# Seven block products in place of eight in four gate-and-up column groups of two feed-forward stages

## What is computed

```python
def swiglu(h, w_in, w_out):
    g, u = split_cols(h @ w_in, (D_FF, D_FF))
    return (jax.nn.silu(g) * u) @ w_out

for layer in range(DEPTH):                     # DEPTH = 2
    g = ln_gains[layer]
    x = x + 0.5 * swiglu(rms_norm(x, g[0]), ffn1_w_in[layer], ffn1_w_out[layer])
```

## Time and profile before

| | before |
|---|---|
| median of three runs | 1864.86 us (1864.74 to 1865.78) |
| the profiled execution: time, span | 1865.1 us, 1862.7 us |
| busy: PE, PE weight loads | 1857.9 us (100%), 1623.7 us (87%) |
| busy: VectorE, ScalarE, POOL | 1310.3 us (70%), 1119.3 us (60%), 369.0 us (20%) |
| TensorE's granted clock | full in all 40 slices |
| first feed-forward stage of the change | its down product begins at 883 us, its groups some 110 us earlier |

### The profile page before, as it was taken

One profiled execution on the slowest core, in us unless ns is written; L12 is line 12 of the kernel. 1 busy time (PEld: TensorE's weight loads), 2 busy tenths in 40 slices (PEclk: granted clock), 3 DMA queues, 4 the chain that ended last, 5 costly groups with the idle time before them and its releaser, 6 DMA issues.

```text
span 1862.7 us, 25413 instructions
## 1 busy us (share of the span) xinstructions
PE 1857.9 (100%) x9293; PEld 1623.7 (87%) x9293; DVE 1310.3 (70%) x1949; ACT 1119.3 (60%) x1678; POOL 369.0 (20%) x606
## 2 busy tenths in 40 slices
PE   9999999999999999999999999999999999999999
PEld 8888988888889888888888889888888888899888
DVE  6776776667777776666577886776666578977664
ACT  6776655557766655555468785654555467765553
POOL 2101233111001431122103001531122111102320
PEclk9999999999999999999999999999999999999999
DMA  9767789878578997798765567997798788758984
GB/s 316 236 186 229 222 258 299 260 233 253 166 221 242 292 287 232 219 272 255 238 180 191 174 191 204 281 274 237 225 255 252 227 265 242 216 157 232 255 258 138
DMA packets 289803, 436.43 MB, mean 234 GB/s; under 512 B 25548, under 2 KB 170416, under 8 KB 289424
## 3 DMA queue, kind: packets, MB, share of 16 engines
q1 hardware_dynamic: 260384, 352.41, 61.9%
q0 software_dynamic: 28832, 82.07, 16.3%
q10 hardware_dynamic: 464, 0.34, 0.1%
HBM read 396.43 MB, written 38.29 MB: 233 GB/s over the span
## 4 chain that ended last, share of the span: by engine, by line
PE 99%; DMA 0%; DVE 0%; SPq 0%; ACT 0%; issue 0%; ACTq 0%
PE M L1081 31%; PE M L1083 31%; PE M L1082 31%; PE AUX L1124 1%; PE AUX L1138 0%; PE AUX L1252 0%; DMA RAW<-in_w_in 0%; PE AUX L1244 0%; PE AUX L1242 0%; PE AUX L1279 0%; PE AUX L1167 0%; PE AUX L1295 0%; PE AUX L1323 0%; PE AUX L1296 0%; PE AUX L1297 0%; PE AUX L1324 0%
## 5 line engine op out<-in xcount | busy, mean ns | idle before, releaser
L1647 DVE TENSOR_TENSOR WL<-RAW,WH 128x1024 fp32r<-128x1024 f32 (+1 forms) x669 | 810.8, 1217 | 383.5 <-ACT WH L1358 380.9
L1358 ACT ACTIVATE WH<-RAW 128x1024 fp32r<-128x1024 f32 (+1 forms) x670 | 705.0, 1055 | 518.8 <-PE M L1083 469.7
L1081 PE MATMUL M<-WH,Bh 128*128 128x512 f32 (+1 forms) x1820 | 691.3, 380 | 0.6 <-ACT TMP L1401 0.3
L1082 PE MATMUL M<-WL,Bh 128*128 128x512 f32 (+1 forms) x1820 | 683.1, 375 | 0.0
L1083 PE MATMUL M<-WH,Bl 128*128 128x512 f32 (+1 forms) x1820 | 683.1, 375 | 0.0
L1081 PEld LDWEIGHTS M<-WH,Bh 128*128 128x128 f32 x1820 | 344.2, 189 | 50.6 <-issue 4.2
L1083 PEld LDWEIGHTS M<-WH,Bl 128*128 128x128 f32 x1820 | 344.2, 189 | 47.1
L1082 PEld LDWEIGHTS M<-WL,Bh 128*128 128x128 f32 x1820 | 344.4, 189 | 44.7
L1396 ACT ACTIVATE AS<-M,KEEP 128x256 f32<-128x256 f32 x132 | 55.3, 470 | 80.3 <-PE M L1083 78.7
L1081 PE MATMUL M<-WH,MTh 128*128 128x512 f32 x128 | 51.0, 398 | 0.0
L1082 PE MATMUL M<-WL,MTh 128*128 128x512 f32 x128 | 48.5, 379 | 0.0
(11 more groups left out here) (534 smaller groups left out, 2886.9 us busy)
## 6 DMA issues: line engine op xcount, KB each, us to landing
RAW<-in_ffn_w_in SPq DMA_DIRECT2D x352, 256.0 KB, 4.2
RAW<-in_w_in SPq DMA_DIRECT2D x103, 512.0 KB, 4.8
RAW<-in_w_gate_up SPq DMA_DIRECT2D x176, 256.0 KB, 4.4
RAW<-in_ffn_w_out SPq DMA_DIRECT2D x88, 512.0 KB, 4.6
RAW<-in_w_down SPq DMA_DIRECT2D x44, 512.0 KB, 4.9
RAW<-in_x_w_kv SPq DMA_DIRECT2D x32, 512.0 KB, 4.6
RAW<-in_even_w_in SPq DMA_DIRECT2D x24, 512.0 KB, 4.5
RAW<-in_odd_w_in SPq DMA_DIRECT2D x24, 512.0 KB, 5.4
```

Of the source, the lines that this page charges most:

```text
L1081: e.matmul(out, s.hi, wh, start=s.at0, stop=False)
L1082: e.matmul(out, s.hi, wl, start=False, stop=False)
L1358: e.activation(hi, raw, ACT.Copy).then_inc(k.w_hi, 1)
L1647: e.tensor_tensor(lo, raw, hi.bitcast(F32), ALU.subtract).then_inc(k.w_lo, 1)
```

## The change

In both stages, groups 6 and 9 of the eleven are computed with seven block products in place of eight. The tokens times features (2 x 2 blocks of 128 tokens by 512 features) and the weights (2 x 2 blocks of 512 features by 256 columns, gate or up) are combined by sums in float32; each product is 128 tokens by 512 features by 256 columns. With all its parts:

- **Weight plan.** `add_mixed` lays group 5's four plain units ("o") and group 6's seven product units ("p") in turn, by `TURNS`; the same for groups 8 and 9. A product unit is four feature blocks by 256 columns and has no load of its own (`None`). TensorE makes 12 matmuls of 256 columns with it (`sp`, `sp2`), into banks of `AUX`.
- **Weight blocks.** SP loads the four blocks of the group into `TMP` (rows 0 to 7), 256 KB a transfer, two transfers after each of the four units that stand before the first product. The first of them waits for the last token sum (first pass) or for the subtraction of the last product unit of the pass before (second pass).
- **Weight sums.** POOL makes T1 to T4 (`tsum`), 1024 elements a partition each, into `KX` and over blocks no longer needed. T1 waits for all eight transfers, T2 for T1 and the subtraction of the first product unit, T4 for T2 and that of the fourth.
- **Token sums.** Once a stage VectorE adds high and low parts back together (2048 elements), POOL makes four sums of 512, ScalarE and VectorE their parts, in rows of `GA` and a new tile `SUM`.
- **Product sums.** `sv0` (ScalarE copy), `sv1` (three on VectorE), `sv2` (one) add up the products; silu and gating of the group then read these instead of `M`.
- **Conversions.** The seven product units are converted from blocks and sums, by the same two operations as before: eleven units in two groups where there were eight.
- The results of groups 8 and 9 are turned into `GA` only after the last product has been used, since the token sums lie there.

```diff
+    def add_mixed(name, w):
+        v = w.rearrange("(k p) (two f) -> p k two f", p=P, two=2)
+        for c in ORDER:
+            if not isinstance(c, tuple):
+                add(name, w, [gu[c]], pairs=True)
+                continue
+            plain, own = c
...
+            for x in TURNS:
+                if x[0] == "o":
+                    q = int(x[1])
+                    units.append((2, 512, v[:, 2 * q:2 * q + 2, :, 256 * plain:256 * plain + 256]))
+                else:
+                    seven["at"].append(len(units))
+                    units.append((4, 256, None))
...
+ORDER = (0, 1, 2, 3, 4, (5, 6), 7, (8, 9), 10)
+TURNS = "p0 o0 p1 p2 o1 p3 p4 o2 p5 o3 p6".split()
+BLOCKS = "B11 B21 B22 T1 T3 T2 T4".split()
...
+        for j, (at, kind) in enumerate(((-7.5, "T1"), (-7.0, "T3"), (-3.0, "T2"), (3.5, "T4"))):
+            s = self.add("tsum", start + at)
...
+        elif s.kind in ("sp", "sp2"):
...
+            for kk in range(4):
+                wh, wl = (woven(x[:, h, 256 * kk:256 * kk + 256]) for x in (p.WH, p.WL))
+                e.matmul(out, xh[kk], wh, start=kk == 0, stop=False)
+                e.matmul(out, xh[kk], wl, start=False, stop=False)
+                i = e.matmul(out, xl[kk], wh, start=False, stop=kk == 3)
+            i.then_inc(k.w_used, 1)
...
+                if j < 3:
+                    e.wait_ge(k.d_sr, 128 * (n + 1))
+                else:
+                    e.wait_ge(k.t_made, 4 * n + j - 2)
+                e.wait_ge(k.w_used, s.u - NHL + 1)
+                e.activation(in_four(p.WH[:, h, 0:s.size]), block(p, BLOCKS[j]), ACT.Copy).then_inc(k.w_hi, 1)
...
+            e.tensor_tensor(pair(p.TMP[8]), pair(p.AUX[x1.bank][:, :]), twice(p.JK[:, 0:256]), ALU.add).then_inc(k.aux_out[x1.bank], 1)
...
+            e.tensor_tensor(pair(p.VT), pair(p.AUX[x3.bank][:, :]), twice(p.TMP[8][:, 256:512]), ALU.add).then_inc(k.part_sum, 1)
...
+            e.tensor_tensor(p.FLAT[:, 512:768], p.AUX[x3.bank][:, 0:256], p.VT[:, 256:512], ALU.add).then_inc(k.aux_out[x3.bank], 1)
+        elif s.kind == "sv2":
...
+        elif s.kind == "tsum":
+            at = p.sevens[s.i]["at"]
+            x, y = {"T1": ("B12", "B11"), "T3": ("B22", "B12"), "T2": ("B22", "T1"), "T4": ("B21", "T2")}[s.what]
+            if s.what == "T1":
+                e.wait_ge(k.d_sr, 128 * (s.i + 1))
+            elif s.what == "T2":
+                e.wait_ge(k.t_made, 4 * s.i + 1)
+                e.wait_ge(k.w_lo, at[0] + 1)
+            elif s.what == "T4":
+                e.wait_ge(k.t_made, 4 * s.i + 3)
+                e.wait_ge(k.w_lo, at[3] + 1)
+            e.tensor_tensor(block(p, s.what), block(p, x), block(p, y), ALU.subtract).then_inc(k.t_made, 1)
...
         weights(i)
+        if i in p.blocks_at:
+            n, q = p.blocks_at[i]
+            x = p.sevens[n]
+            if q == 0 and n % 2 == 0:
+                e.wait_ge(k.s_lo, 4 * (n // 2) + 4)
+            elif q == 0:
+                e.wait_ge(k.w_lo, p.sevens[n - 1]["at"][6] + 1)
+            for j in range(2):
+                e.dma_start(p.ROWS[:, 2 * q + j, :].rearrange("p (two f) -> p two f", two=2), x["src"][q][:, j]).then_inc(k.d_sr, 16)
```

More of the change, by code:

```diff
@@ L531, in residual, with token_sums, seven_products, ffn @@
             x.after = self.n_unit
-    def ffn(self, gate, down, lab_in, lab_mid, scale, gain, lab_next, A, HB, final=False, gated=False, early=None):
+    def token_sums(self, lab, A, extra):
+        n = self.n_seven // 2
+        s = self.add("sums", self.now + 0.6)
+        s.i, s.done = n, self.n_unit
+        s.makers = []
+        for kt in range(KD):
+            if self.made[lab, kt] not in s.makers:
+                s.makers.append(self.made[lab, kt])
+        s.hi, s.lo = ([x[:, 16 + 2 * i:18 + 2 * i, :].rearrange("p k c -> p (k c)") for i in range(3)] for x in A)
+        s.hi.append(extra[:, 0:512])
+        s.lo.append(extra[:, 512:1024])
+        self.add("sums_hi", self.now + 12.0).s = s
+        return s
+    def seven_products(self, gate, lab, sums, c_):
+        i = self.n_seven
+        self.n_seven += 1
+        c, tiles = None, []
+        start = self.now
+        for j, (at, kind) in enumerate(((-7.5, "T1"), (-7.0, "T3"), (-3.0, "T2"), (3.5, "T4"))):
+            s = self.add("tsum", start + at)
+            s.i, s.j, s.what = i, j, kind
+        for x in TURNS:
+            q = int(x[1])
+            if x[0] == "o":
+                c = self.chunk(gate, self.B, 0, KD, lab, span=(2 * q, 2 * q + 2), c=c, last=q == 3)
+                continue
+            u = self.unit(gate)
+            assert self.part[u] == (i, q)
+            s = self.add("sp2" if q in LEADS else "sp", self.now, 3)
+            s.u, s.i, s.q, s.sums = u, i, q, sums
+            s.lead = tiles[LEADS[q]] if q in LEADS else s
+            tiles.append(s)
+            self.now += 1.0
+            if q in (0, 5):
+                s = self.add("sv0" if q == 0 else "sv1", self.now)
+                s.i, s.tiles = i, tiles
+        s = self.add("sv2", self.now, 0)
+        s.i, s.tiles = i, tiles
+        return c, s
+    def ffn(self, gate, down, lab_in, lab_mid, scale, gain, lab_next, A, HB, final=False, gated=False, early=None, extra=None):
         flat = [x[:, :, :].rearrange("p a c -> p (a c)") for x in HB]
@@ L551, in ffn @@
             s.past = out[i].last
-            self.split(c.end + 0.1, c.end + 12.6, "ff", s, s.h, [out[i]], [back[i]], A, 2 * c_, None, lab_mid, 2 * c_)
+            x = self.split(s.at + 0.1, s.at + 12.6, "ff" if c is not None else "parts", s, s.h, [out[i]], [back[i]], A, 2 * c_, None, lab_mid, 2 * c_)
+            if extra is not None and c_ == 0:
+                sums = self.token_sums(lab_in, A, extra)
+            if extra is not None and c_ >= 8:
+                x.after = self.n_unit if c_ < 10 else 0
         room = [Rows(flat[1])] + out, [Rows(flat[2])] + back
@@ L1641, in vector @@
             h = s.u % NHL
[L1642 removed]
+            hi, lo = p.WH[:, h, 0:s.size], p.WL[:, h, 0:s.size]
+            if s.u in p.part:
+                e.wait_ge(k.w_hi, s.u + 1)
+                e.tensor_tensor(in_four(lo), block(p, BLOCKS[p.part[s.u][1]]), in_four(hi.bitcast(F32)), ALU.subtract).then_inc(k.w_lo, 1)
+                continue
+            raw = p.RAW[:, p.slot[s.u], 0:s.size]
             if s.ncol < 256:
```

204 lines of the change are left out of this document (163 added, 41 removed).

## The result

| | us |
|---|---|
| before, median of 4 runs on the same chip | 1864.8 (1864.46 to 1865.78) |
| after, median of 4 runs | 1902.62 (1901.06 to 1903.81) |
| after over before | 1.020, 95% interval 1.0188 to 1.0213 |
| span of the profiled execution after | 1900.9 |

The change made the kernel 38 us slower; whether by less or more than 2% the interval leaves open. The prediction was 1892.0, with a range of 1866 to 1926 and 1882 to 1905 for its likeliest case.

A forecast was written before the change was run, and what follows sets the result against it. TensorE's own work and waits were taken as the bound: 1865.1 - 3.9 saved + 2 x (7.6 in the gap + 7.8 in the second pass) = 1892.0 us; range 1866 to 1926, likeliest case 1882 to 1905 (chance 0.45).

The forecast's parts named there:

- What bounds the kernel.: Whole kernel: TensorE's matmuls are busy for the whole span, so its own work and any wait forced on it count.
- TensorE, 3.9 saved.: Matmuls of the two groups: seven products cost 9.37 us against a group's 10.35, saving 0.98 a pass, 3.9 in all.
- The rival by which products are not cheaper: Switches between product and plain unit: slower matmuls take 0.8 of the 0.98 us saved a pass; 1864.5 without waits; within-3.7-us outcome 0.09.
- Token sums.: Groups 1 to 3 of each stage: they cost TensorE nothing; SP goes on at about 29 us, due at 25.6.
- POOL's sum, taken as 2.8.: POOL's block sums of 1024 elements: 2.8 us each, by POOL's own rate, between bounds of 1.22 and 3.9.
- The first pass is in time.: First pass, begun by TensorE at S: T1 from S - 6.5, last product converted at S + 17.0, wanted at S + 18.4.
- The lead of 8.0 covers that: Stage start: conversions are ready 8.0 us early, which covers SP's going on at about 29 us instead of 25.6.
- a sum need not meet a subtraction: POOL's block sums: most of a sum need not run beside a VectorE subtraction, so 2.8 us is taken, not 3.9.
- The gap, 7.6.: Group 7, between passes: SP holds weights behind the second pass's blocks; TensorE waits 3.0, 0.9, 2.8 and 0.9, together 7.6 us.
- The second pass, 7.8 before the last product.: Second pass: POOL's queue of sums and exchanges ends its last conversion at 26.2, wanted at 18.4; TensorE waits 7.8 us.
- The rival "shut each other out": The lock: VectorE yields to POOL's whole sums, 15.1 us a stage on top, 1922 in all; chance 0.22.
- No clock below full is expected.: TensorE's clock in the profile after: stays at full throughout, so slowed matmuls are charged 0.

The follow-up runs named there:

- experiment 5: Changed kernel with the second pass's block transfers behind group 7's weights and POOL's sums cut to 8 elements (output not the reference's): 1861.71 us.
- experiments 11 and 12: Run 9's kernel with token sums behind two conversions and their ScalarE conversions later: 1865.02 us; the same with only group 6 by seven products: 1867.12 us.
- run 9: Changed kernel, block and token sums on VectorE, each block sum just ahead of its conversion, second pass's blocks behind group 7's third and fourth loads: 1863.45 us.
- run 10: As run 9, but with the token sums left on POOL: 1865.14 us.
- Experiment 1: Changed kernel with the second pass's block transfers moved behind the last load of group 7's weights in SP's queue: 1888.97 us.
- experiment 3: Changed kernel with each POOL block sum replaced by two constant fills that read nothing (output not the reference's): 1886.74 us.
- experiment 4: Changed kernel with only group 6 of each stage by seven products, groups 8 and 9 as in the kernel before: 1877.67 us.
- experiment 6: Changed kernel with block sums on VectorE in place of POOL and the second pass's block transfers behind group 7's weights: 1870.48 us.
- experiments 7 and 8: Changed kernel with block sums on VectorE, transfers where the change has them: 1883.87 us; the same with only group 6 by seven products: 1870.15 us.

## Why the prediction was right in sign, and 10.6 us short

- *What bounds the kernel.* Right: the whole loss appears as waits of TensorE, and the rest of its time is unchanged.
- *TensorE, 3.9 saved.* Right. Matmuls of 256 columns start 0.11 apart; experiment 5 shows 4.2, and experiments 11 and 12 differ by 2.1 for two passes of 0.98. The rival by which products are not cheaper falls: it had 1864.5 for a kernel without waits.
- *Token sums.* The term of TensorE was right (no wait there), the reason incomplete. On POOL they take 2.14 to 2.27 us each, hardly less than block sums twice their size (2.37): beside them four subtractions of VectorE take 7.87 us from 787.56. They end at 801.5 instead of 799, and SP waits 2.3 us for them; but the first blocks begin no earlier than 801.26 in run 9 either, where the sums are long done and SP's loads wait for VectorE. Run 9 against run 10, one execution each, puts 1.7 us on the sums' place, by way of the exchanges.
- *POOL's sum, taken as 2.8.* Measured 2.35 to 2.41 undisturbed. The estimate of 2.25 from the Trainium skill (GPSIMD Engine Reference, 3.1 Elementwise) was closer than mine from POOL's medians. Its total, 1883, was further off, because the length was not the failing term.
- *The first pass is in time.* This is the step that failed. T1 began with S (821.75 for S = 821.7), not at S - 6.5: it stands behind group 3's way out, that waits for group 3's gating, and the gating, forecast as in the kernel before, was 7.3 us later (818.88 for 811.59), behind conversions whose weights came late between the blocks. "The lead of 8.0 covers that" was checked for TensorE alone, and not for what else stands in the same orders. The last product's conversion ended at S + 22.1, not 17.0. And "a sum need not meet a subtraction" does not hold where VectorE has hardly a free moment (busy for 23.2 of 25 us from 815 to 840): the first two sums are back to back, and the subtraction that they catch lasts 6.05 us. First pass: 4.9 and 4.0 us of idle time in place of none.
- *The gap, 7.6.* Right in place and mechanism, 6.0 and 6.8 in size. Experiment 1 proves it by removing the transfers alone.
- *The second pass, 7.8 before the last product.* 5.1 and 4.9, and none of it at the last product. In the second stage nearly all is at the first plain unit (a step of 4.67), whose subtraction waits for two POOL sums (6.07 us from 1437.99): what I had put on POOL's queue is there the lock. In the first stage nearly all is at the third plain unit (4.61): there POOL's queue is late, as forecast, but because two sums took 5.44 and 3.36 us beside VectorE, and it is felt through the ways back and not through T4. Right term, wrong place, and a cause that is only in part the one given.
- *The rival "shut each other out".* It had 0.22, as all or nothing at 15.1 us a stage beyond the forecast. It is true as a mechanism and much smaller in effect, up to 8 us a stage (experiment 3), because a stretched subtraction costs only what the lead doesn't cover. Its price should have been an addend to the likeliest case: forecast and rival were no alternatives.
- *"No clock below full is expected."* Wrong, and this is nearly the whole error: the slow steps are 9.9 of 10.6 us, some 8.6 of them at the lower clock. The forecast idle time, 15.4 us a stage, is what was measured (16.0 and 15.7), by errors that cancel, which is luck; that idling also slows the matmuls behind it was no term of the sum at all.

## What to carry to other kernels

In this kernel elementwise work on GpSimd didn't relieve a busy VectorE where both read SBUF: a block sum of 1.2 us on VectorE cost less than one of 2.4 on POOL (1870.5 against 1889.0 with the same queue of SP). Late transfers can also cost where TensorE doesn't wait, by all that stands behind the late conversions in the engines' orders. A transfer whose buffer comes free late must not stand in a queue ahead of transfers whose buffers are free; that order alone was worth 13 us, three times what the change could give. And each wait of TensorE is to be reckoned with the slow matmuls that can follow it.

## What the runs showed of the hardware that was not expected

- **The clock falls after an idle stretch and stays down for some us.** The table lists, over four kernels, TensorE's ten longest steps in these stages; each is followed by matmuls 0.43 us apart (or 0.22 at 256 columns) before the step is 0.2157 again.

| kernel | longest steps, us | slow steps behind each |
|---|---|---|
| after | 4.63, 4.61, 3.85, 4.67 | 9, 8, 8, 13 |
| experiment 1 | 4.63, 4.18, 6.45 | 6, 11, 13 |
| experiment 3 | 5.25, 4.01 | 6, 8 |
| experiment 4 | 4.63 | 15 |

Between 2 and 3.6 us both are seen: 2.18 in experiment 1 was followed by 8 slow steps, 2.51 in experiment 4 by 6 and 3.51 in experiment 6 by 7, which begin 1.2 us behind its end; but 3.51 in experiments 7 and 8, and 2.41, 2.47 and 2.40 in the gaps of the changed kernel, by none. In the changed kernel it is 0.3 us of lost clock for each 1 us of waiting (9.9 to 31.7).

- **The lock runs over two operations.** The subtraction of 821.46 did not go ahead between the two sums; it waited for both (6.05 us, where one sum costs it 3.90 in all, at 837.62). It is seen the other way too: beside VectorE's work a block sum on POOL took up to 5.44 us, at 865.11, and ended 2.25 us, about its own time, behind the last of three subtractions (864.83 to 868.30).

- **Who waits can't be read from who starts first.** By the records a subtraction begins 0.29 us ahead of the sum at 821.46 and 0.30 ahead at 1437.99, and it is the subtraction that waits; at 864.83 it begins 0.28 ahead, and POOL waits. POOL's records are rough in time, so what decides stays open.
